# Position-bias step compares and their matmuls between the k steps of the second feed-forward (one core)

## What is computed

```python
def _swiglu(x, w_gate, w_up, w_down):            # feed-forward, 1024 -> 2816 -> 1024
    return (jax.nn.silu(x @ w_gate) * (x @ w_up)) @ w_down
...
h = _rmsnorm(x, ffn2_norm[layer])
x = x + 0.5 * _swiglu(h, ffn2_w_gate[layer], ffn2_w_up[layer], ffn2_w_down[layer])
return _rmsnorm(x, final_norm)                   # end of the first block
...
proj = h @ w_in                                  # head of the second block
dq, dk, dv, cq, ckv, kr, g = jnp.split(proj, ...)
...
bucket = _t5_bucket(positions[:, None, :] - qpos[:, :, None])
bias = jnp.transpose(rel_bias[bucket], (0, 3, 1, 2))      # 4 heads x 512 x 512
logit_d = jnp.where(allowed, logit_d + bias, NEG_INF_2)
```

## Time and profile before

| what | value |
|---|---|
| median of 3 runs | 2228.06 us (2227.45 to 2228.09) |
| profiled execution | span 2227.2 us, first to last instruction; no other time of it is given |
| PE busy | 1973.1 us, 89% of the span, 9093 matmuls |
| DVE busy | 1105.9 us, 50% |
| ACT busy | 606.5 us, 27% |
| POOL busy | 591.4 us, 27% (571.1 us of it `w_lo`) |
| chain that ended last | PE 72%, DVE 21% |
| second feed-forward, about | 1337 us to 1701 us of the span |
| head of the second block, slots 0 to 11 | about 1720 us to 1886 us |

### The profile page before, as it was taken

One profiled execution on the slowest core, in us unless ns is written; L12 is line 12 of the kernel. 1 busy time (PEld: TensorE's weight loads), 2 busy tenths in 40 slices (PEclk: granted clock), 3 DMA queues, 4 the chain that ended last, 5 costly groups with the idle time before them and its releaser, 6 DMA issues.

```text
span 2227.2 us, 22783 instructions
## 1 busy us (share of the span) xinstructions
PE 1973.1 (89%) x9093; PEld 1555.2 (70%) x9093; DVE 1105.9 (50%) x1762; ACT 606.5 (27%) x936; POOL 591.4 (27%) x154
## 2 busy tenths in 40 slices
PE   1999999899679999998799889999997798579799
PEld 1788888678557667875588767888885576356477
DVE  3664111373357776635700247311115777787971
ACT  2321221211025554103522223212223212124450
POOL 0444443341000001303144424444432211020232
PEclk6999999998769999999899989999998999699999
DMA  4345332330100000212133322333322111110221
GB/s 126 133 160 190 114 95 65 119 117 20 56 0 1 1 1 20 85 36 88 53 99 95 95 80 76 90 90 114 95 80 81 57 57 63 36 39 15 62 76 57
DMA packets 246249, 163.60 MB, mean 73 GB/s; under 512 B 22256, under 2 KB 237440, under 8 KB 246016
## 3 DMA queue, kind: packets, MB, share of 16 engines
q1 hardware_dynamic: 231712, 157.91, 23.2%
q10 hardware_dynamic: 14432, 4.24, 0.8%
HBM read 155.84 MB, written 6.29 MB: 73 GB/s over the span
## 4 chain that ended last, share of the span: by engine, by line
PE 72%; DVE 21%; issue 2%; ACT 2%; ACTq 1%; POOL 1%; DMA 0%; DVEq 0%; SPq 0%
PE bank L755 18%; PE bank L756 18%; PE bank L757 18%; PE bank L932 3%; DVE rs L1256 3%; PE bank L956 3%; PE bank L942 2%; DVE step L1590 2%; ACTq L561 1%; PE bank L916 1%; DVE rout L1552 1%; DVE tmp L1230 1%; DVE bank L1649 1%; DVE mstat L1652 1%; PE bank L812 1%
## 5 line engine op out<-in xcount | busy, mean ns | idle before, releaser
L445 POOL TENSOR_TENSOR w_lo<-w_raw,w_hi 128x2048 fp32r<-128x2048 f32 (+3 forms) x134 | 571.1, 4262 | 1519.5 <-ACT w_hi L501 1519.5
L755 PE MATMUL bank<-h_hi,w_hi 128*128 128x512 f32 x1280 | 521.2, 407 | 53.7 <-DVE h_lo L1223 36.6
L756 PE MATMUL bank<-h_lo,w_hi 128*128 128x512 f32 x1280 | 504.1, 394 | 0.0
L757 PE MATMUL bank<-h_hi,w_lo 128*128 128x512 f32 x1280 | 503.6, 393 | 0.0
L501 ACT ACTIVATE w_hi<-w_raw 128x2048 fp32r<-128x2048 f32 (+3 forms) x134 | 236.8, 1767 | 687.2 <-PE bank L757 622.4
L755 PEld LDWEIGHTS bank<-h_hi,w_hi 128*128 128x128 f32 x1280 | 244.3, 191 | 122.8 <-issue 45.9
L756 PEld LDWEIGHTS bank<-h_lo,w_hi 128*128 128x128 f32 x1280 | 244.3, 191 | 58.0 <-issue 8.5
L757 PEld LDWEIGHTS bank<-h_hi,w_lo 128*128 128x128 f32 x1280 | 243.9, 191 | 52.2
L1366 DVE TENSOR_TENSOR act_f<-silu,bank 128x512 f32<-128x512 f32 x44 | 30.3, 688 | 295.5 <-PE bank L757 295.4
L755 PE MATMUL bank<-u_hi,w_hi 128*128 128x512 f32 x352 | 138.3, 393 | 0.0
L756 PE MATMUL bank<-u_lo,w_hi 128*128 128x512 f32 x352 | 138.0, 392 | 0.0
(11 more groups left out here) (321 smaller groups left out, 2897.1 us busy)
## 6 DMA issues: line engine op xcount, KB each, us to landing
w_raw<-in_w_in SPq DMA_DIRECT2D x28, 1024.0 KB, 5.2
w_raw<-in_ffn_w_gate SPq DMA_DIRECT2D x44, 512.0 KB, 3.8
w_raw<-in_ffn_w_up SPq DMA_DIRECT2D x44, 512.0 KB, 4.8
w_raw<-in_ffn_w_down SPq DMA_DIRECT2D x32, 704.0 KB, 4.5
ada_w<-in_ada_w SPq DMA_DIRECT2D x16, 768.0 KB, 6.1
w_raw<-in_w_in SPq DMA_DIRECT2D x21, 512.0 KB, 4.1
w_raw<-in_w_out SPq DMA_DIRECT2D x8, 1024.0 KB, 5.1
w_raw<-in_w_branch_nsa SPq DMA_DIRECT2D x8, 512.0 KB, 5.1
```

The costliest lines, as they stand in the source:

```text
L445: pool.tensor_sub(w_lo[s % 2][:, 0:n], w_raw[s % 2][:, 0:n], w_hi[s % 2][:, 0:n]).then_inc(s_lo, 1)
L755: pe.matmul(o, l[0], r[0], start=first, stop=False)
L756: pe.matmul(o, l[0], r[1], start=False, stop=False)
L757: return pe.matmul(o, l[1], r[0], start=False, stop=last)
```

## The change

The compares, their matmuls and the bout copies leave the 12 slots of the head. `per_tile` gives each slab of the second feed-forward a number of groups: none in up slabs 0 to 5 of the first half, 5 in each of up slabs 6 to 10, 3 in each of the 8 down tiles, then 5 in each of the 11 up slabs and 3 in each of the 8 down tiles of the second half (25 + 24 + 55 + 24 = 128). PE does a group ahead of an odd k step (k = 1, 3, 5 of a gate or down tile, k = 1, 3 of an up tile). DVE computes the compares of a slab after it has handled the slab before. ACT copies a full bank to `bout` one slab later. The two squares buffers move to 50 to 57 KB of the arena, since steps are alive while they are used.

```diff
-        sqg = [at(f"sqg{i}", [P, S], F32, ARENA + (60 + 2 * i) * KB) for i in range(2)]
-        sqgsum = at("sqgsum", [P, S], F32, ARENA + 64 * KB)
-        rs2 = at("rs2", [P, S], F32, ARENA + 66 * KB)
+        sqg = [at(f"sqg{i}", [P, S], F32, ARENA + (50 + 2 * i) * KB) for i in range(2)]
+        sqgsum = at("sqgsum", [P, S], F32, ARENA + 54 * KB)
+        rs2 = at("rs2", [P, S], F32, ARENA + 56 * KB)
...
-        BIAS_SLOTS = 12
-        bias_groups = lambda i: range(P * i // BIAS_SLOTS, P * (i + 1) // BIAS_SLOTS) if i < BIAS_SLOTS else range(0)
+        per_tile = [0] * 6 + [5] * (HALF_F - 6) + [3] * KD + [5] * HALF_F + [3] * KD
+        bias_ends = np.cumsum(per_tile).tolist()
+        bias_groups = lambda q: range(bias_ends[q] - per_tile[q], bias_ends[q]) if q < len(per_tile) else range(0)
...
 # ACT
+            def evacuate_bias(q):
+                for b in bias_groups(q - 1) if q else range(0):
+                    if b % 8 == 7:
+                        t = b // 8
+                        act.wait_ge(sem("bmm"), b + 1)
+                        if t >= 2:
+                            act.wait_ge(sem(f"bias_stored{t % 2}"), 16 * (t // 2))
+                        act.activation(bout[t % 2][:, :], bank[6 + t % 2][:, :], ACT.Copy).then_inc(sem("bias_out"), 1)
+                        act.wait_ge(sem("bias_out"), t + 1)
+                        act.dma_start(bias_dram[...], bout[t % 2][:, :]).then_inc(sem(f"bias_stored{t % 2}"), 16)
...
                         tick(act.activation(silu[m % 2][:, :], bank[a % 4][:, :], ACT.Silu), "act_gate")
+                        if f == "ffn2":
+                            evacuate_bias(i // 2 + (0 if a < first_acc["ffn2_down0"] else HALF_F + KD))
+                def down(half):
+                    squares = square_before(n) if half else nothing
+                    def work(i, a):
+                        squares(i, a)
+                        if f == "ffn2":
+                            evacuate_bias(HALF_F + i + half * (HALF_F + KD))
+                    return work
...
             ffn("ffn2", 3)
+            evacuate_bias(len(per_tile))
             big_norm(3)
...
 # PE
-            def feature_tile(wh, wl, k0, kt, cols, src, width=P, ready=None):
+            def feature_tile(wh, wl, k0, kt, cols, src, width=P, ready=None, groups=()):
                 o = open_acc()
+                groups = list(groups)
                 for k in range(kt):
+                    if k % 2 == 1 and groups:
+                        bias_step(groups.pop(0))
                     if ready:
...
+            def bias_step(i):
+                t, g = i // 8, i % 8
+                if i == 0:
+                    pe.wait_ge(sem("win_ready"), 1)
+                    pe.wait_ge(sem("lam_exp"), 1)
+                pe.wait_ge(sem("step_ready"), i + 1)
+                if g == 0 and t >= 2:
+                    pe.wait_ge(sem("bias_out"), t - 1)
+                w = slice(112 - 16 * g, 240 - 16 * g)
+                pe.matmul(bank[6 + t % 2][:, :], win_hi[:, w], step[i % 4][:, :], start=g == 0, stop=False)
+                pe.matmul(bank[6 + t % 2][:, :], win_lo[:, w], step[i % 4][:, :], start=False, stop=g == 7).then_inc(sem("bmm"), 1)
...
                 if n == 3:
+                    pe.wait_ge(sem("bias_out"), 15)
                     pe.matmul(bank[6][:, :], ones, sqgsum[:, :], start=True, stop=True).then_inc(sem("gmm"), 1)
...
-                        feature_tile(wh, wl, 0, KD, slice(0, P), (h_hi, h_lo))
-                        feature_tile(wh, wl, KD, KD, slice(0, P), (h_hi, h_lo))
+                        groups = bias_groups(m + half * (HALF_F + KD)) if f == "ffn2" else ()
+                        feature_tile(wh, wl, 0, KD, slice(0, P), (h_hi, h_lo), groups=groups[0:3])
+                        feature_tile(wh, wl, KD, KD, slice(0, P), (h_hi, h_lo), groups=groups[3:])
...
-                        feature_tile(wh, wl, 0, HALF_F, slice(0, P), (u_hi, u_lo), ready=("hid_ready", hid0) if m == 0 else None)
+                        feature_tile(wh, wl, 0, HALF_F, slice(0, P), (u_hi, u_lo), ready=("hid_ready", hid0) if m == 0 else None,
+                                     groups=bias_groups(HALF_F + m + half * (HALF_F + KD)) if f == "ffn2" else ())
...
 # DVE
+            def bias_steps(q):
+                for i in bias_groups(q):
+                    if i >= 4:
+                        dve.wait_ge(sem("bmm"), i - 3)
+                    tick(dve.tensor_scalar(step[i % 4][:, :], posb, thr[:, i:i + 1], None, ALU.is_ge), "step_ready")
...
                         if f == "ffn2" and half == 0:
                             prepare(m)
+                        if f == "ffn2":
+                            bias_steps(m + 1 + half * (HALF_F + KD))
...
+                        if f == "ffn2":
+                            bias_steps(HALF_F + m + 1 + half * (HALF_F + KD))
...
 # head of the second block: the bias work in the slots' beside() is gone on PE, DVE and ACT
-                for i in bias_groups(slot):
-                    bias_steps(i)
...
-                bias_steps(slot + 1)
...
-            bias_steps(0)
```

More of the change, by code:

```diff
@@ L478, in build @@
                      **{27 + h: [14 + h] for h in range(4)}}
-        BIAS_SLOTS = 12
-        bias_groups = lambda i: range(P * i // BIAS_SLOTS, P * (i + 1) // BIAS_SLOTS) if i < BIAS_SLOTS else range(0)
+        per_tile = [0] * 6 + [5] * (HALF_F - 6) + [3] * KD + [5] * HALF_F + [3] * KD
+        bias_ends = np.cumsum(per_tile).tolist()
+        assert bias_ends[-1] == P
+        bias_groups = lambda q: range(bias_ends[q] - per_tile[q], bias_ends[q]) if q < len(per_tile) else range(0)
         rope_bank = lambda j: bank[4 + j % 2] if j < 19 else bank[4]
@@ L584, in _ @@
             act.activation(sc_f[:, :], col[:, G_C:G_C + KD], ACT.Silu).then_inc(sem("c_silu"), 1)
+            def evacuate_bias(q):
[7 more added lines that the diff above has]
+                        act.wait_ge(sem("bias_out"), t + 1)
+                        act.dma_start(bias_dram[:, 32 * t:32 * t + 32, :].rearrange("h q k -> q h k"), bout[t % 2][:, :]).then_inc(sem(f"bias_stored{t % 2}"), 16)
             def ffn(f, n):
@@ L595, in gate @@
                         tick(act.activation(silu[m % 2][:, :], bank[a % 4][:, :], ACT.Silu), "act_gate")
+                        if f == "ffn2":
[7 more added lines that the diff above has]
+                    return work
                 for half in range(2):
                     each_slab(f"{f}_up{half}", gate, 2)
-                    each_slab(f"{f}_down{half}", square_before(n) if half else nothing, 1)
+                    each_slab(f"{f}_down{half}", down(half), 1)
             def prepare(i):
@@ L686, in _ @@
             split_h(3)
-            def store_bias(i):
-                act.wait_ge(sem("bias_out"), i + 1)
-                act.dma_start(bias_dram[:, 32 * i:32 * i + 32, :].rearrange("h q k -> q h k"), bout[i % 2][:, :]).then_inc(sem(f"bias_stored{i % 2}"), 16)
             def beside(slot0):
@@ L695, in work @@
                     slot = slot0 + i
[L696 to L704, removed]
                     for j in NORM_SLOT.get(slot, []):
@@ L1040, in _ @@
             big_norm(3)
[L1041 to L1052, removed]
             slot_at = [0]
@@ L1584, in _ @@
             make_h(3, G_MOD + 8, G_MOD)
[L1586 to L1590, removed]
             slot_at = [0]
```

## The result

The changed kernel takes 2391.72 us (median of 4, 2388.66 to 2394.19) against 2228.07 us: a ratio of 1.0731, 95% interval 1.0716 to 1.0746. The forecast was 2400 us in a range of 2350 to 2430.

A forecast was written before the change was run, and what follows sets the result against it. PE was taken to bound the second feed-forward and DVE the head of the second block. Against a 2227.2 us span, matmuls +58, waits +142, clock +53 and head -81 gave +172: 2400 us, range 2350 to 2430.

The forecast's parts named there:

- Matmuls added: Second feed-forward: 256 bias matmuls at 0.226 us each all count, as PE has no idle time there; +58 us.
- Waits: Second feed-forward: PE waits for each group's first compare, late in DVE's queue and often held by POOL's `w_lo`; +142 us.
- Clock: Second feed-forward: PE runs at 1.2 GHz after 22 waits of 5 us or more, 2.4 us lost each; +53 us.
- Head: Head of the second block: without the bias the first `qm` copy comes at 1812 instead of 1893.1; -81 us.
- B: Second feed-forward: the first compare beats POOL's `w_lo`, giving two shorter waits a slab; 2365 us, chance 0.10.
- C: Second feed-forward: POOL doesn't hold compares, so only queue order costs, 56 us, with no slow clock; 2260 us, chance 0.06.
- D: Second feed-forward: PE finds each group ready at k = 1, so no waits, a gain of 23 us; 2204 us, chance 0.04.

The follow-up runs named there:

- the filler: The changed kernel with 19 to 26 matmuls without use ahead of each of the 22 long waits: 2349.09 us, ratio 1.0546 to the kernel before.

## Why the prediction was right, step by step

- **Matmuls added** (+58, bounds 56 to 60). Too low by 6, and outside its own bounds: 0.497 us a group makes 64 for 128. With bias matmuls in it, PE's stream without a gap held 438 matmuls in 100 us (0.2283 us each) where it held 531 in 120. Why the mixed stream is 1% slower was not tried and stays open.
- **Waits** (+142). Measured 136 as idle time, 140 with the restarts. Every kind came out: 6.4 against 6.6 us, 4.9 against 5.05, 4.9 against 5.2, 0.66 against 0.9, and in the right number, 13, 4, 5 and 10. (In slab 6 the wait was right for another reason: `prepare`'s operation was held, and not the compare.) The sizes came from a look-alike in the same place, the tensor-scalar of slab 2. The runs with POOL waiting, from PSUM, and with the compares first each take one leg of the mechanism away and the wait shrinks as it should.
- **Clock** (+53, bounds 35 and 64). 43 by the filler, the largest miss. The prediction took 2.4 us a wait, between its two samples of 1.6 and 2.9 and "nearer the second"; it was 1.9, nearer the first. That waits of this length are followed by the slow clock was right for all 22.
- **Head** (-81). -79.5. From PE's restart in cq's second slab to the first `qm` copy it took 70.7 us, where 69 were forecast. Behind it came -3.1 that the sum didn't have. Of this 1.8 is a collision that moved: the last two `dkz` products, held by a `w_lo` for 4.94 us before, take 3.18 now, as that `w_lo` starts 2.66 us ahead of them and not 0.89. The rest I did not trace.
- The misses, +6, -2, -10, +1.5 and -3, make -7.5 us; the median is 8.3 under the forecast. So the total is somewhat closer than its largest term, as the matmuls' miss happened to take off more than half of the clock's.
- **Rivals.** B (the compare first) didn't occur: in the slabs looked at POOL was ahead of the first compare by 0.02 to 0.56 us (in the last down tile both are drawn at the same time), and no slab shows two long waits. The chance of 0.10 can't be judged from that, as the order was the same each time. C was built twice. Its waits are right (54 against 56), its time was 31 us off, and the failed step is "with no slow clock", which holds 24 of the 31. D, the gain, was put to a mechanism that the code excludes; with the compares moved ahead it is real, at -19 us instead of -23, short mainly by the matmuls' 6.

## What to carry to other kernels

Work put between the k steps of a stage where PE is the bound has to be ready before PE gets there, all of it, and not only in the mean: with 22 of 120 us busy on the producer, 17 compares that came late behind `u_lo` still made PE wait for more than 100 us. Look in the trace for what already runs in the place where the new operation is to go; its duration there, not its median, is the price. Where another engine's work, begun 0.03 us ahead, holds an operation, the order of the queue or the memory it reads from is worth more than its length: over the 22 long waits here, moving a compare of 0.48 us up in the queue saved 7.0 us a wait, and reading it from PSUM 4.1.

## What the runs showed of the hardware that I had not expected

- TensorE went back to 1.2 GHz after idle times as short as 1.98 us that came once a slab; in the run where POOL waited, 11 of 14 up slabs stood 17.1 us apart and three 15.5. The gaps of 1.0 us every 2.7 us in the norm ahead of the head, in the kernels before and after, were not followed by it, nor were the waits of 0.8 us once a slab in the run with compares first.
- Busy work pays: 19 to 26 matmuls without use ahead of each long wait made the kernel 1.8% faster.
- A compare from PSUM costs 0.74 us against 0.48 from SBUF, but none of the 128 was held beside POOL's work (0.752 at most); the one from SBUF took up to 4.84. A tiny operation is held as long: one on 128 x 1 elements took 4.45, against 0.15 for the tensor-scalars of that size right behind it.
